# First half of an output product moved ahead of the block's end in a fused two-block model on one core

## The reference

```
h = x
for i in (0, 1):
    u     = rmsnorm(h, norm_g[i])
    p     = u @ w_in[i]                      # 8 pieces of 512 columns: q, k of 2 head groups, v, z
    q, k  = head-wise rmsnorm and rotary of their pieces
    o     = masked softmax attention, 8 heads of 128, 512 x 512
            (even: 4 heads of differential attention and 4 with a forget gate;
             odd: 8 heads with a dilated pattern)
    mixed = o * silu(z)                      # even, first group: o also normed and scaled
    h     = h + mixed @ w_out[i]
    h     = h + sigmoid(h @ w_ple_gate[i]) * embeds[i]
```

## Time and profile before

| what | value |
|---|---|
| median of 3 runs | 2508.7 us (2507.11 to 2510.89) |
| the profiled execution | 2509.27 us, span 2507.4 us |
| granted clock, mean | 0.964 |
| PE busy | 2265.2 us (90%) |
| DVE, ACT, POOL busy | 1020.3 (41%), 627.2 (25%), 236.3 us (9%) |
| DMA | 578.95 MB, mean 231 GB/s |

### The profile page before, as it was taken

How to read it: one execution, slowest core, us unless ns; L and a number is a source line. 1 busy time by engine, 2 the same in 40 slices (tenths; PEclk the granted TensorE clock), 3 DMA queues, 4 the chain that set the end, 5 groups by cost and what they waited for, 6 DMA issues and landing times. The chain is left out here.

```text
span 2507.4 us, 31530 instructions
## 1 busy us (share of the span) xinstructions
PE 2265.2 (90%) x12172; PEld 1503.5 (60%) x12172; DVE 1020.3 (41%) x1822; ACT 627.2 (25%) x1316; POOL 236.3 (9%) x285
## 2 busy tenths in 40 slices
PE   4999989889987999998989898987999989999989
PEld 2877669589864434343434343433677768787877
DVE  3577625735663121112111111104654655664345
ACT  4442224344431111010101010100343341323321
POOL 5233324800010000000000000000000000000000
PEclk8999999899987999999999999999999999999999
DMA  6114655754266999999999999997321113332131
GB/s 231 51 54 138 219 173 198 195 144 113 86 234 264 417 417 418 417 418 418 418 418 418 418 418 418 418 417 276 128 79 55 51 74 112 124 101 67 35 134 51
DMA packets 214544, 578.95 MB, mean 231 GB/s; under 512 B 65976, under 2 KB 100769, under 8 KB 180769
## 3 DMA queue, kind: packets, MB, share of 16 engines
q1 hardware_dynamic: 206264, 564.18, 59.1%
q0 software_dynamic: 2496, 8.40, 0.9%
q10 hardware_dynamic: 5673, 4.83, 0.6%
HBM read 544.86 MB, written 32.51 MB: 230 GB/s over the span
## 5 line engine op out<-in xcount | busy, mean ns | idle before, releaser
L1778 PE MATMUL ps_gate_up<-expert_ring,pair_columns 128*64 128x512 f32 x1024 | 461.3, 603 | 58.5 <-DMA expert_ring<-in_moe_w_up_dram 50.7
L1779 PE MATMUL ps_gate_up<-expert_ring,pair_columns 128*64 128x512 f32 x1024 | 462.4, 604 | 0.0
L1778 PEld LDWEIGHTS ps_gate_up<-expert_ring,pair_columns 128*64 128x64 f32 x1024 | 136.1, 138 | 346.4 <-issue 343.9
L2089 DVE TENSOR_TENSOR hidden_tokens<-silu_gate,ps_gate_up 64x512 f32<-64x512 f32 x64 | 42.3, 690 | 512.9 <-ACT silu_gate L1970 512.4
L1765 PE MATMUL ps_down<-expert_ring,hidden_columns 128*64 128x512 f32 x512 | 228.1, 596 | 2.3 <-DMA expert_ring<-in_moe_w_down_dram 2.3
L1766 PE MATMUL ps_down<-expert_ring,hidden_columns 128*64 128x512 f32 x512 | 228.1, 596 | 0.0
L1765 PEld LDWEIGHTS ps_down<-expert_ring,hidden_columns 128*64 128x64 f32 x512 | 66.8, 137 | 134.6 <-issue 120.7
L1779 PEld LDWEIGHTS ps_gate_up<-expert_ring,pair_columns 128*64 128x64 f32 x1024 | 136.2, 139 | 0.0
L769 DVE SCALAR_TENSOR_TENSOR conv_out<-conv_in,tap_columns,conv_out 128x770 f32<-128x770 f32 (+1 forms) x96 | 120.2, 1252 | 3.4
L120 PE MATMUL even_bank<-stream_high,columns_high 128*128 128x512 f32 x256 | 109.4, 427 | 10.6 <-PEq L92 6.8
L114 DVE TENSOR_TENSOR stream_low<-stream_raw,stream_high 128x2048 fp32r<-128x2048 f32 x48 | 110.1, 2293 | 1.6
(11 more groups left out here) (552 smaller groups left out, 4352.9 us busy)
## 6 DMA issues: line engine op xcount, KB each, us to landing
expert_ring<-in_moe_w_gate_dram SPq DMA_DIRECT2D x128, 1024.0 KB, 22.6
expert_ring<-in_moe_w_up_dram SPq DMA_DIRECT2D x128, 1024.0 KB, 23.8
expert_ring<-in_moe_w_down_dram SPq DMA_DIRECT2D x128, 1024.0 KB, 19.7
win_ring<-in_gdn_w_in_dram SPq DMA_DIRECT2D x16, 1024.0 KB, 8.2
late_mod_ring<-in_w_mod_dram SPq DMA_DIRECT2D x16, 1024.0 KB, 5.8
stream_raw<-in_w_in_even_dram SPq DMA_DIRECT2D x16, 1024.0 KB, 5.3
stream_raw<-in_w_in_odd_dram SPq DMA_DIRECT2D x16, 1024.0 KB, 5.3
stream_raw<-in_w_ple_gate_dram SPq DMA_DIRECT2D x8, 1024.0 KB, 5.2
```

The lines of the kernel that those rows point to most:

```text
L1778: mm(psA[LO, c], xe[:, e, k], ex.gate_up[s0][:, j, cols], start=(k == 0), stop=(k == KC - 1))
L1779: last = mm(psA[HI, c], xe[:, e, k], ex.gate_up[s1][:, j, cols], start=(k == 0), stop=(k == KC - 1))
L2089: nc.vector.tensor_tensor(hid[HI, c % 2], sg[HI, c % 2], psA[HI, c], ALU.mult).then_inc(hidden, 1)
```

## The change

In both layers' attention stages heads 0 to 3 are turned in steps N and N + 1 of the loop, two in each, with their high and low parts right there on ACT and DVE. After the loop PE waits for the four lows, does the first half of the output product (piece 16, four token tiles), and turns heads 4 to 7 between the second and the third tile. DVE splits piece 17 before it gates heads 4 to 7. `layer_outputs` begins with the second pass. For this the eight banks are allocated once for both layers.

SP issues the loads of pieces 3 to 5 before the store of the residual, in both layers. DVE makes the forget weights' parts before it norms the residual. The scratch rows of the norm values move to a tile of `layer_tokens`, and `final_norms` has two rows left.

```diff
@@ -2202,6 +2202,7 @@
         m.sb("second_block_place", [P, SecondBlock.SIZE // 4])
         assert nc.sbuf_base == second.place + SecondBlock.SIZE
         h_dram = [nc.dram_tensor(f"residual_kept{i}", [P, LT, D], F32, kind="Internal").ap() for i in range(2)]
+        second.bank = [m.ps(f"second_bank{i}", [P, COLS]) for i in range(8)]
         for i in range(2):
             layer_tokens(nc, dram, per, second, i * second.layer, i == 0, h_dram[i])
             layer_outputs(nc, dram, per, second, i * second.layer + 16, i, h_dram[i], out)
@@ -2235,6 +2236,7 @@
     with Mem(nc) as m:
         sb = lambda name, shape: m.sb(f"{tag}_{name}", shape)
         work = sb("token_work", [P, 10 * D])
+        nss = sb("norm_small", [P, 3, LT])
         mask_raw, mask_parts, ident_r = sb("mask_rows", [P, SEQ]), sb("mask_parts", [P, 1 if even else 2, SEQ]), sb("ident_rounded", [P, P])
         qkT = sb("head_columns", [P, HEADPIECES, 4, SEQ])
         vec = sb("rows", [P, 2 * A_DIM + 3 * B_DIM + 4 * A_DIM if even else 2 * P])
@@ -2274,7 +2276,7 @@
             KINDS = [(vec[:, 0:P], P, 16, P ** -0.5)] * 2 + [(vec[:, P:2 * P], P, 16, 1.0)] * 2
         mask_at = 0 if even else SEQ
         mask = [mask_parts[:, i] for i in range(1 if even else 2)]
-        bank = [m.ps(f"{tag}_bank{i}", [P, COLS]) for i in range(8)]
+        bank = second.bank
 
         sem = lambda name: m.sem(f"{tag}_{name}")
         vectors_in, mask_in, h_stored, map_zeroed = sem("vectors_in"), sem("mask_in"), sem("h_stored"), sem("map_halves_zeroed")
@@ -2296,10 +2298,13 @@
                 for dst, src in vectors:
                     sp.dma_start(dst, src, allow_slow_non_contiguous=True).then_inc(vectors_in, 16)
                 sp.dma_start(mask_raw[:, :], dram["attn_const"][:, mask_at:mask_at + SEQ]).then_inc(mask_in, 16)
+                early = G0 + 2 * stream.SLOTS
+                for g in range(G0 + stream.SLOTS, early):
+                    stream.load(sp, g)
                 if even:
                     sp.wait_ge(h_normed, LT)
                 sp.dma_start(h_dram, h[:, :, :]).then_inc(h_stored, 16)
-                for g in range(G0 + stream.SLOTS, G0 + 2 * PIECES + stream.SLOTS):
+                for g in range(early, G0 + 2 * PIECES + stream.SLOTS):
                     stream.load(sp, g)
                 sp.wait_ge(h_stored, 16)
 
@@ -2408,7 +2413,7 @@
                     pe.wait_ge(mixed, j + 1)
                     if j == 0:
                         pe.wait_ge(moved, PIECES * LT)
-                    if j == 4:
+                    if j == HK:
                         pe.wait_ge(p_kept, N)
                         pe.wait_ge(taken, N)
                         pe.wait_ge(exped, upto(N - 1))
@@ -2447,8 +2452,16 @@
                         turn_probs(n - 2)
                     if n >= 3:
                         attend(n - 3)
-                for j in range(KC):
-                    turn_mixed(j)
+                    if n in (N, N + 1):
+                        for j in range(2 * (n - N), 2 * (n - N) + 2):
+                            turn_mixed(j)
+                for t in range(LT):
+                    if t == 0:
+                        pe.wait_ge(m_low, HK)
+                    if t == 2:
+                        for j in range(HK, KC):
+                            turn_mixed(j)
+                    stream.product(pe, G0 + 2 * PIECES, t, bank[t][:, :], X)
 
             @block.scalar
             def _(act):
@@ -2507,6 +2520,10 @@
                     for t in range(LT):
                         nc.scalar.activation(z[:, g, t], z[:, g, t], ACT.Silu).then_inc(silu_done, 1)
 
+                def mixed_high(j):
+                    act.wait_ge(mturned, j + 1)
+                    nc.scalar.activation(XH[:, j].bitcast(F32R), bank[j][:, :], ACT.Copy).then_inc(m_high, 1)
+
                 for k in range(HK, KC):
                     act.wait_ge(xturned, k - HK + 1)
                     nc.scalar.activation(XH[:, k].bitcast(F32R), bank[k][:, :], ACT.Copy, scale=gain[:, k:k + 1]).then_inc(x_high, 1)
@@ -2516,12 +2533,12 @@
                         n = i * LT + t
                         if n >= 2:
                             act.wait_ge(squared_x, n - 1)
-                        nc.scalar.activation(xsq[:, n % 2], x[:, t], ACT.Square, accum_out=norms[:, 2 + i, t:t + 1]).then_inc(squared_x, 1)
+                        nc.scalar.activation(xsq[:, n % 2], x[:, t], ACT.Square, accum_out=nss[:, i, t:t + 1]).then_inc(squared_x, 1)
                 act.wait_ge(squared_x, LT * len(squares))
-                nc.scalar.activation(norms[:, 4], norms[:, 2], ACT.Sqrt, scale=1.0 / D, bias=per["eps"][:, 0:1]).then_inc(rooted_x, 1)
+                nc.scalar.activation(nss[:, 2], nss[:, 0], ACT.Sqrt, scale=1.0 / D, bias=per["eps"][:, 0:1]).then_inc(rooted_x, 1)
                 if even:
                     act.wait_ge(ratio, 1)
-                    nc.scalar.activation(norms[:, 4], norms[:, 3], ACT.Sqrt, scale=1.0 / D, bias=per["eps"][:, 0:1]).then_inc(rooted_x, 1)
+                    nc.scalar.activation(nss[:, 2], nss[:, 1], ACT.Sqrt, scale=1.0 / D, bias=per["eps"][:, 0:1]).then_inc(rooted_x, 1)
                 act.wait_ge(inverted, 1)
                 head_moves(0)
                 if even:
@@ -2567,10 +2584,12 @@
                             act.wait_ge(osums, 4)
                             nc.scalar.activation(oss[:, 1], oss[:, 0], ACT.Sqrt, scale=1.0 / P, bias=per["eps"][:, 0:1]).then_inc(orooted, 1)
                         silu(0)
+                    if n in (N, N + 1):
+                        for j in range(2 * (n - N), 2 * (n - N) + 2):
+                            mixed_high(j)
                 silu(1)
-                for j in range(KC):
-                    act.wait_ge(mturned, j + 1)
-                    nc.scalar.activation(XH[:, j].bitcast(F32R), bank[j][:, :], ACT.Copy).then_inc(m_high, 1)
+                for j in range(HK, KC):
+                    mixed_high(j)
 
             if even:
                 @block.gpsimd
@@ -2682,6 +2701,10 @@
                     dve.wait_ge(silu_done, (g + 1) * LT)
                     nc.vector.tensor_tensor(out[g][:, hh], out[g][:, hh], z[:, g, :, hh * P:(hh + 1) * P], ALU.mult).then_inc(mixed, 1)
 
+                def mixed_low(j):
+                    dve.wait_ge(m_high, j + 1)
+                    nc.vector.tensor_tensor(XL[:, j].bitcast(F32R), bank[j][:, :], XH[:, j], ALU.subtract).then_inc(m_low, 1)
+
                 stream.part(dve, G0 + 1)
                 low_of(range(HK, KC))
                 dve.wait_ge(mask_in, 16)
@@ -2689,24 +2712,24 @@
                 seq(take_high(nc, mask_parts[:, 0], mask_raw[:, :]))
                 dve.wait_ge(rooted_x, 1)
                 if even:
-                    seq(nc.vector.reciprocal(norms[:, 0], norms[:, 4]))
-                    seq(nc.vector.tensor_tensor(norms[:, 3], norms[:, 3], norms[:, 0], ALU.mult))
-                    nc.vector.tensor_tensor(norms[:, 3], norms[:, 3], norms[:, 0], ALU.mult).then_inc(ratio, 1)
+                    seq(nc.vector.reciprocal(norms[:, 0], nss[:, 2]))
+                    seq(nc.vector.tensor_tensor(nss[:, 1], nss[:, 1], norms[:, 0], ALU.mult))
+                    nc.vector.tensor_tensor(nss[:, 1], nss[:, 1], norms[:, 0], ALU.mult).then_inc(ratio, 1)
                     dve.wait_ge(rooted_x, 2)
-                    seq(nc.vector.reciprocal(norms[:, 1], norms[:, 4]))
+                    seq(nc.vector.reciprocal(norms[:, 1], nss[:, 2]))
                     nc.vector.tensor_tensor(norms[:, 1], norms[:, 1], norms[:, 0], ALU.mult).then_inc(inverted, 1)
                 else:
-                    nc.vector.reciprocal(norms[:, 0], norms[:, 4]).then_inc(inverted, 1)
+                    nc.vector.reciprocal(norms[:, 0], nss[:, 2]).then_inc(inverted, 1)
                 stream.part(dve, G0 + 2)
                 if even:
+                    nc.vector.memset(sub[:, 6:8], 0.0).then_inc(misc, 1)
+                    dve.wait_ge(vectors_in, 16 * len(vectors))
+                    seq(take_high(nc, gh[:, :, :], gw[:, :, :]))
+                    take_low(nc, gl[:, :, :], gw[:, :, :], gh[:, :, :]).then_inc(misc, 1)
                     dve.wait_ge(fg_loaded, 16)
                     for t in range(LT):
                         nc.vector.scalar_tensor_tensor(out=h[:, t], in0=h[:, t], scalar=norms[:, 0, t:t + 1], in1=fg,
                                                        op0=ALU.mult, op1=ALU.mult).then_inc(h_normed, 1)
-                    nc.vector.memset(sub[:, 6:8], 0.0).then_inc(misc, 1)
-                    dve.wait_ge(vectors_in, 16 * len(vectors))
-                    seq(take_high(nc, gh[:, :, :], gw[:, :, :]))
-                    take_low(nc, gl[:, :, :], gw[:, :, :], gh[:, :, :]).then_inc(misc, 1)
                 else:
                     take_low(nc, mask_parts[:, 1], mask_raw[:, :], mask_parts[:, 0]).then_inc(misc, 1)
                 for n in range(HEADPIECES):
@@ -2748,12 +2771,15 @@
```

(15 more changed lines are left out.)

## The result

The changed kernel takes 2465.41 us (median of four executions, of which one took 3873 us at a mean clock of 0.55 and is left out of the ratio). The kernel before, timed beside it, takes 2508.26: ratio 0.9829, 95% interval 0.9811 to 0.9847, so 43 us less. The forecast was 2485, at lowest 2478. The profiled execution took 2465.14, its span 2463.2.

The account below looks back on a forecast made before the run. PE, busy 90% of the span, was taken as the bound. Tails of 7.7 and 8.5 us plus the start's 5.9 and 1.8 of clock sum to 23.9 off 2509.27, forecast as 2485 us; range 2478 to 2496.

Parts of the forecast that it names:

- Small values elsewhere: Norm values and the smaller final_norms, which shifts later tiles some tens of bytes lower: taken as 0 us.
- a rival below: Expert stage: new addresses make each row's landing cost more, so the kernel gets slower, 2515 us; chance 0.04.
- The tail: Attention's end, both layers: the moved output half gains 7.7 us in the even layer and 8.5 in the odd one.
- the walk: Engine-by-engine timing of the even layer's new attention end: second output half starts at 2060.7 instead of 2068.4, gaining 7.7 us.
- Piece 19: Output stage: its weights land 17.1 us after the start, split at 20.6, needed at 23.8; no cost, 3.2 us margin.
- The start: Even layer's start: waits of 3.8 and 2.0 us go, 5.9 us together, plus 1.8 us of clock.
- the 3.8 us hole: PE's wait for a stream_low piece at the even layer's start: goes whole, and the half behind it keeps 1.8 us of clock.
- The forget product's 1.7: Even layer's start: 1.7 us lost to low clock in the forget product, left as it is, no gain counted.
- The clock stays low: Rival: closing PE's holes does not restore the clock; 2491 us, or 2487 to 2489 if some gains fail; chance 0.20.
- DVE becomes the bound: Rival for the tail: late DVE lows, takes or split, or piece 19 2 us late, give 2489 us; chance 0.13.
- Moved, not filled: Rival for the tail: PE waits for low 3 as long as now, only the start's 7.7 remains; 2501 us, chance 0.06.

Follow-up runs that it names:

- tail_only: The changed kernel with the old order at the layer's start and final_norms at five rows, leaving only the moved output half: 2494.77 us, ratio 0.9937.
- head_only: The kernel before with only the loads moved ahead of the residual's store and the forget parts ahead of the norming: 2495.78 us, ratio 0.9946.
- turns_after_loop: The changed kernel with turns, highs and lows of heads 0 to 3 after the attention loop instead of inside it: 2471.74 us, ratio 0.9847.
- split_last: The changed kernel with DVE's split of piece 17 behind the last four lows instead of ahead of the gates: 2464.58 us, ratio 0.9817.
- norms_only: The kernel before with only final_norms cut to two rows and its scratch in a layer tile, later tiles 64 bytes lower: 2493.88 us, ratio 0.9932.
- before_up_192: The kernel before with an unused 192-byte tile ahead of the rope tables, putting the expert ring at 40704: 2492.96 us, ratio 0.9932.
- ring_up_192: The kernel before with 192 unused bytes between small and large tiles, moving only the large ones, expert ring at 40704: 2493.45 us, ratio 0.9929.
- small_down_64: norms_only with 64 bytes of padding behind the small tiles, putting the ring and large tiles back at 40512: 2510.16 us, ratio 0.9999.
- loads_first: The kernel before with only the loads of pieces 3 to 5 ahead of the residual's store, in both layers: 2500.02 us, ratio 0.9955.

## Why the prediction was right or wrong

**Small values elsewhere, taken as 0: this step failed.** "Every tile allocated after it starts some tens of bytes lower. No row shows another placement, so I take 0, bounded by a rival below." That rival went one way only: new addresses could hurt the expert stage. The case that they help was not priced at all, though the old place was as unexamined as the new one and the stage had the same lack of slack in both directions.

The ring's start went from 40512 bytes, 64 past a multiple of 256, to 40448, a multiple. The stage that loads 384 MB of weights then took 940 us instead of 957, and 16 to 17 of the 20 missing us are this. Where the effect would act and what it would be worth were right (the loads set the pace, 961 us, 1% of rate is 10 us); its sign and its chance of 4% were not. The rival's own words, that each row's landing at a shifted address costs more, held for the old address: 4.6 and 4.3 ns a row.

The Trainium skill (DMA: Bandwidth & Descriptors, How a descriptor splits into AXI transactions) points the same way. It says that a descriptor is split into transactions of 256 bytes, and that one which doesn't start at a multiple of 256 has its first transaction begin at the boundary below. It says this of bytes that are fetched, and gives no time for it; of writes into SBUF, which is where the place changed here, it says nothing. If it holds for them, an estimate from that section is 33 transactions instead of 32 for a row of 8192 bytes and 17 instead of 16 for one of 4096. One more per row, whatever its length and whatever the offset, is the pattern that the packets show. In size it is less than in proportion: 4.6 ns where a 32nd of 309 would be 9.7. No run here counted transactions.

**The tail: right.** Set against PE's turn at 2042.16 before and 2013.74 after, the walk's times move down by 28.42: first product 2019.08 (came 2019.13), second half of the output product 2032.28 (2032.41). Odd layer 8.5, came 8.4; both alone 16.2, came 15.9. ACT's silus end at 2021.7 as walked. The prediction has the turns of heads 4 to 7 paced by the gates, though by its own times the gates are done early enough; PE found each head ready as it came to it (1.91 us for 16). tail_only has the lower clock for 33.8 us of its second block instead of 42.3, worth 4.3 us in all, where the forecast had 1.7 and 2.5.

**Piece 19: right.** It was walked to land 17.1 us after the output stage's first product and did so by 15.3:

```profile
2047.74 1.23 DVE L110 CAST stream_high<-stream_raw 128x2048 fp32r<-128x2048 f32 x1 [3.48 <-DMA stream_raw<-in_w_out_even_dram]
```

DVE now waits for it, 3.5 us, where it had not waited before. It has it split 18.9 us after that product, 4.9 before the 23.8 at which PE was to want it.

**The start: waits right, clock too small.** Both waits went whole. The forecast was 5.9 + 1.8 = 7.7. From the block's first product to the turn at 2013.74 are 279.3 us, before 291.7: 12.4 came, and head_only gave 14.9. The term that was mis-sized is the clock, 1.8 against 6.5, and by head_only's trace 8.6. Only the half behind the 3.8 us hole was counted. The forget product's 1.7 was left out; without its hole it ran at 1.00. And at the forget rows and behind them the lower level lasts 3.4 us instead of 10.2, though neither kernel has a hole above 0.3 us just ahead of them. Windows of PE after, over the forget product, then over the end of the forget rows with the first products, then 6.0 us further on:

```profile
1755.00:1770.00 15.00, 15.00 (x70) 1.00 0.67 236
...
1830.50:1836.30 5.80, 5.80 (x20) 0.71 0.59 184
1836.30:1842.30 6.00, 6.00 (x29) 1.00 0.00 1
```

**The rivals.** "The clock stays low" went the other way: no low clock in the new products, 16 transposes between them included, as the windows of the tail show. The Trainium skill (TensorE: Matmul & The Clock Gate, Part 4: PE-mode transpose) says that transposes don't count for the clock as matmuls do; with 1.9 us of them between products and no hole beside them this cost nothing here. turns_after_loop shows that this rival was near: with 1.9 us of transposes and 1.9 us of hole behind them the clock fell to 0.55 for 3.4 us. Of the 4.5 us lost 2.8 are the longer waits of both layers (3.8 against 1.0). "DVE becomes the bound" fell with split_last: 3.5 us of DVE work can stand on either side of the gates. "Moved, not filled" fell with tail_only.

## What to carry to other kernels

When an edit changes a tile's size, write down which later tiles move and where large DMA destinations start modulo 256 bytes. In a stage whose DMA engines were full, a start at a multiple was worth 1.8% of its time here, and one pad of some bytes bought it. The price was per row, so shorter rows paid more in proportion (2.7% for 4096 bytes, 1.5% for 8192). An unknown bounded on the loss side needs a bound on the gain side from the same rows. And a hole on PE costs its length and the clock behind it: the start's two holes were 5.9 us, and closing them won 14.9.

## What the runs showed of the hardware that was not expected

- Large DMAs (1 MB, 8192 bytes per partition, all DMA engines full) run at 425 to 426 GB/s into tiles that start at a multiple of 256 bytes, and at 416 to 419 GB/s at offsets 32, 64 and 128 (windows of 100 us from 1000 us on). A row of 8192 bytes takes 309.1 ns against 313.7, one of 4096 bytes 159.0 against 163.3.
- The clock falls in much the same places in the profiles of norms_only, before_up_192 and before, counted from the second block's start, though that start is 15 to 16 us earlier in the first two than in the last. It falls in other places once work ahead is moved. So it follows the program more than chance; in ring_up_192 and small_down_64, which have the same second block but for the scratch tile, some of its places were other ones, so not wholly. Why the forget rows and the products behind them keep more of their clock after the reordering stays open.
- loads_first scattered by 11 us between five executions of one chip, where the other changed kernels scattered by 2 to 8 and the kernel before by up to 12 in 17. The cause wasn't looked for.
